# Eighteen early score units, two value units loaded ahead, and cross attention with a PSUM bank for each head

## The reference

```python
def chunk(xc):                                        # PEER: 16384 experts
    q = (xc @ w_query).reshape(PEER_CHUNK, PEER_HEADS, 2, PEER_HALF)
    s1, s2 = ...                                      # scores against 2 x 128 sub-keys
    v1, i1 = lax.top_k(s1, PEER_TOPK)
    v2, i2 = lax.top_k(s2, PEER_TOPK)
    ...
    top, ci = lax.top_k(cand, PEER_TOPK)
    gate = jax.nn.softmax(top, axis=-1)
    act = jax.nn.gelu(jnp.einsum('td,thkd->thk', xc, u))
    return jnp.einsum('thk,thkd->td', gate * act, vv)

def memory_cross_attention(h, m, w_q, w_kv, w_o):     # 4 heads of 256
    s = jnp.einsum('bshd,bmhd->bhsm', q, k) * (XATTN_HEAD_DIM ** -0.5)
    p = jax.nn.softmax(s, axis=-1)
    o = jnp.einsum('bhsm,bmhd->bshd', p, v).reshape(bsz, seq, D_MODEL)
    return jnp.einsum('bse,ed->bsd', o, w_o)
```

## Time and profile before

| what | value |
|---|---|
| median of 3 runs | 2027.73 us (2023.18 to 2029.29) |
| the profiled execution | 2019.04 us, of which the span of its instructions is 2017.4 us |
| PE busy | 1853.8 us (92%) |
| DVE busy | 1341.3 us (66%) |
| ACT busy | 910.5 us (45%) |
| chain that ended last | PE 82%, DVE 9%, ACT 3% of the span |

### The profile page before, as it was taken

The page is one execution under the profiler, slowest core; times in us unless marked ns, Lnnn a source line. Parts: engine busy times, 40 slices in busy tenths (PEclk is TensorE's granted clock), DMA queues, the critical chain, the costliest instruction groups (busy, mean ns, idle before and its releaser), DMA issues.

```text
span 2017.4 us, 25894 instructions
## 1 busy us (share of the span) xinstructions
PE 1853.8 (92%) x10094; PEld 1580.2 (78%) x10094; DVE 1341.3 (66%) x1876; ACT 910.5 (45%) x967; POOL 76.5 (4%) x99
## 2 busy tenths in 40 slices
PE   5999976999799899999999999888977899999997
PEld 3778744788698679999999999787966678878875
DVE  5688775759897555555555555647953478888885
ACT  2543433411233344444444444445543457666664
POOL 0000000000000331110000000000000000000000
PEclk9999997999899999999999999898988899999999
DMA  6655443434345775666555555544334178888892
GB/s 270 240 178 204 149 144 135 167 108 145 116 148 200 236 239 192 213 206 215 186 187 187 187 187 187 197 155 152 126 117 188 55 293 327 327 343 330 319 350 106
DMA packets 60847, 403.93 MB, mean 200 GB/s; under 512 B 7921, under 2 KB 8337, under 8 KB 14305
## 3 DMA queue, kind: packets, MB, share of 16 engines
q1 hardware_dynamic: 51504, 371.22, 50.6%
q0 software_dynamic: 5808, 20.29, 3.4%
q10 hardware_dynamic: 3458, 11.37, 1.7%
HBM read 390.79 MB, written 12.06 MB: 200 GB/s over the span
## 4 chain that ended last, share of the span: by engine, by line
PE 82%; DVE 9%; ACT 3%; issue 3%; DMA 3%; SPq 0%; ACTq 0%; DVEq 0%
PE ps L2152 21%; PE ps L2153 21%; PE ps L2154 21%; PE ps L2254 7%; PE ps L2530 3%; ACT whi L630 2%; DVE wlo L1125 2%; DMA raw<-in_stream_dram 1%; DMA X<-in_x_dram 1%; PE ps L2702 1%; PE ps L2767 1%; PE ps L2589 1%; PE ps L2183 1%; PE ps L2397 1%; PE ps L2629 1%
## 5 line engine op out<-in xcount | busy, mean ns | idle before, releaser
L1125 DVE TENSOR_TENSOR wlo<-raw,whi 128x2048 fp32r<-128x2048 f32 x186 | 429.6, 2310 | 394.0 <-ACT whi L630 394.0
L630 ACT ACTIVATE whi<-raw 128x2048 fp32r<-128x2048 f32 x186 | 356.2, 1915 | 395.0 <-PE ps L2154 372.1
L2152 PE MATMUL ps<-thi,whi 128*128 128x256 f32 x1088 | 310.6, 285 | 9.5 <-DVE wlo L1125 7.0
L2153 PE MATMUL ps<-tlo,whi 128*128 128x256 f32 x1088 | 309.9, 285 | 0.0
L2154 PE MATMUL ps<-thi,wlo 128*128 128x256 f32 x1088 | 309.8, 285 | 0.0
L2152 PE MATMUL ps<-whi,phi 128*128 128x512 f32 x608 | 242.9, 400 | 21.9 <-DVE plo L1705 15.6
L2152 PE MATMUL ps<-whi,thi 128*128 128x512 f32 (+1 forms) x584 | 232.5, 398 | 20.1 <-DVE tlo L1137 11.7
L2153 PE MATMUL ps<-wlo,phi 128*128 128x512 f32 x608 | 240.8, 396 | 0.0
L2154 PE MATMUL ps<-whi,plo 128*128 128x512 f32 x608 | 239.9, 395 | 0.0
L2154 PE MATMUL ps<-whi,tlo 128*128 128x512 f32 (+1 forms) x584 | 228.4, 391 | 0.0
L2153 PE MATMUL ps<-wlo,thi 128*128 128x512 f32 (+1 forms) x584 | 228.1, 391 | 0.0
(11 more groups left out here) (403 smaller groups left out, 2624.2 us busy)
## 6 DMA issues: line engine op xcount, KB each, us to landing
raw<-in_stream_dram SPq DMA_DIRECT2D x264, 1024.0 KB, 4.8
BIG<-in_stream_dram SPq DMA_DIRECT2D x83, 1024.0 KB, 7.0
BIG<-g_spill POOLq DMA_DIRECT2D x64, 128.0 KB, 4.7
BIG<-in_stream_dram SPq DMA_DIRECT2D x2, 2048.0 KB, 15.5
g_spill<-H ACTq DMA_DIRECT2D x4, 1024.0 KB, 4.8
g_spill<-MOD ACTq DMA_DIRECT2D x4, 1024.0 KB, 4.8
MID<-in_gains_dram POOLq DMA_DIRECT2D x7, 512.0 KB, 4.1
s_spill<-MOD ACTq DMA_DIRECT2D x10, 256.0 KB, 4.9
```

The source lines that it names most:

```text
L630: nc.scalar.activation(whi[:, u % 2, :], raw[:, u % 2, :], ACT.Copy).then_inc(unit_hi, 1)
L1125: nc.vector.tensor_tensor(wlo[:, u % 2, :], raw[:, u % 2, :], whi[:, u % 2, :].bitcast(f32), ALU.subtract).then_inc(unit_split, 1)
L2152: nc.tensor.matmul(out, ahi, bhi, start=start, stop=False)
L2153: nc.tensor.matmul(out, ahi, blo, start=False, stop=False)
```

## The change

There are three edits. In all names below, line numbers of the changed kernel differ (L2306 there is L2254 here, L1159 is L1125, L1736 is L1702, L1743 is L1705, L649 is L630, L920 is L899).

First, EARLY goes from 16 to 18. Ten score units (FIRST) now come before the steps that build G, eight between them as before. The ninth and tenth use banks 0 and 1. The tenth is cut in halves, one ahead of the transposes of the routing and one behind; the transposes get three banks. The loop keeps 46 pairs.

Second, the first two value units are loaded into `spare`, which lies in the place of wlo (the allocation is closed at once, so wlo takes the same memory; wlo is idle during the whole units). DVE now multiplies by G ahead of lo, and v(1) is split ahead of phi of v(0).

Third, each head of the cross attention has a bank (4 + h) for its scores, transposes and values in turn, and its own x_p and x_pT. The heads run between the query units and the first W_O unit.

```diff
-EARLY, KEPT = 16, 6
+EARLY, KEPT = 18, 6
+FIRST = EARLY - 8
...
+        with nc.sbuf_tensor("spare", [P, 2, UW], f32) as spare_tensor:
+            spare = spare_tensor
         wlo = sb("wlo", [P, 2, UW], f32r)
...
+        def early_bank(i):
+            return 4 + i % 2 if i < FIRST - 2 else i % 2
...
+        APART = (at_v(0), at_v(1))
...
+                if u in APART:
+                    sp.wait_ge(raw_loaded[u % 2], landed(u - 2))
+                    sp.dma_start(spare[:, u % 2, :], stream[apart[u], :, :]).then_inc(raw_loaded[u % 2], 16)
+                    continue
+                if u - 2 in APART:
+                    sp.wait_ge(raw_loaded[u % 2], landed(u - 2))
+                    sp.wait_ge(unit_used, u - 4 - SPLIT_U + 1)
...
             for i in range(EARLY):
-                if i == 1:
-                    lo(at_v(1))
-                if i >= 2:
-                    lo(at_v(i))
                 if i >= KEPT:
                     dve.wait_ge(s_loaded[(i - KEPT) % 4], 16 * ((i - KEPT) // 4 + 1))
-                gated(i, buffers=(early_out(i), early_out(i)))
+                weighted(i, buffers=(early_out(i), early_out(i)))
+                if i:
+                    lo(at_v(i))
+                weighted_low(i, source=early_out(i))
...
+            for i in range(FIRST - 1):
+                if i >= 2 and early_bank(i) == early_bank(i - 2):
                     pe.wait_ge(gelu_done, i - 1)
-                whole_T(ps[:, 4 + i % 2, :], at_u(i))
-            pe.wait_ge(gelu_done, NE)
+                whole_T(ps[:, early_bank(i), :], at_u(i))
+            whole_T(ps[:, early_bank(FIRST - 1), :], at_u(FIRST - 1), (0, 1))
+            pe.wait_ge(gelu_done, FIRST - 2)
             pe.wait_ge(routed, TT)
             for q in range(3):
-                if q == 2:
-                    pe.wait_ge(route_in, 1)
...
+            whole_T(ps[:, early_bank(FIRST - 1), :], at_u(FIRST - 1), (2, 3))
...
+            group_T(N_XQ, U_XQ, T_HX)
+            group_T(N_XQ + 1, U_XQ + 1)
             x_scores(0)
+            group_T(N_XQ + 2, U_XQ + 2)
             x_scores(1)
+            x_transposes(0)
+            group_T(N_XQ + 3, U_XQ + 3)
+            x_scores(2)
+            x_transposes(1)
+            x_values(0)
+            x_values(1)
+            x_scores(3)
+            x_transposes(2)
+            pe.wait_ge(xo_lo, 2)
+            rows_part(N_XO, U_XO, 0, 0)
+            x_transposes(3)
+            x_values(2)
+            x_values(3)
+            rows_part(N_XO, U_XO, 0, 1)
             pe.wait_ge(xo_lo, XH)
-            for b in range(2):
-                block_rows(N_XO + 2 * b, U_XO + 2 * b, ends=b == 1)
+            block_rows(N_XO, U_XO, units=(1,))
+            block_rows(N_XO + 2, U_XO + 2, ends=True)
```

More of the change, by code:

```diff
@@ L465, in half_cols, with raw_of @@
             return slice(h * 512, (h + 1) * 512)
+        APART = (at_v(0), at_v(1))
+        def raw_of(u):
+            return spare[:, u % 2, :] if u in APART else raw[:, u % 2, :]
         block = ctx.enter_context(nc.Block())
@@ L629, in hi @@
                     act.wait_ge(unit_used, s - 1 + off)
-                nc.scalar.activation(whi[:, u % 2, :], raw[:, u % 2, :], ACT.Copy).then_inc(unit_hi, 1)
+                nc.scalar.activation(whi[:, u % 2, :], raw_of(u), ACT.Copy).then_inc(unit_hi, 1)
             def used(u, off=0):
@@ L1005, in x_out @@
                 nc.scalar.activation(thi[:, 2 * h:2 * h + 2, :].rearrange("p c t -> p (c t)"),
-                                     ps[:, 6 + h % 2, :], ACT.Copy).then_inc(xo_hi, 1)
-            x_exp(0)
-            for i in range(XH * TT):
-                h, t = i // TT, i % TT
-                if i + 1 < XH * TT:
-                    x_exp(i + 1)
-                act.wait_ge(heads_tr, B_HEADS + i + 1)
-                nc.scalar.activation(x_pT[h % 2][:, :, t * P:(t + 1) * P],
-                                     ps[:, 4 + i % 2, 0:S].rearrange("p (k t) -> p k t", k=TT),
-                                     ACT.Copy).then_inc(heads_trT, 1)
-                if t == TT - 1 and h:
-                    x_out(h - 1)
-            x_out(XH - 1)
+                                     ps[:, 4 + h, :], ACT.Copy).then_inc(xo_hi, 1)
+            hi(U_XQ + 2)
+            x_query(0)
+            hi(U_XQ + 3)
+            x_query(1)
+            x_exp(0)
+            hi(U_XO)
+            x_query(2)
+            x_exp(1)
+            x_copy(0)
+            x_query(3)
+            x_copy(1)
+            x_exp(2)
+            x_out(0)
+            x_out(1)
+            hi(U_XO + 1)
+            x_exp(3)
+            x_copy(2)
+            x_copy(3)
+            x_out(2)
+            x_out(3)
             for u in range(U_XO, U_MOE - 2):
@@ L1695, in _, with weighted @@
             dve.wait_ge(g_free, 2 * S // GT)
-            def gated(i, off=0, place=None, buffers=None):
+            def weighted(i, off=0, place=None, buffers=None):
                 place = 2 * (i if place is None else place)
@@ L1703, in gated, with weighted_low @@
                                         G[:, bass.ds(place + 2 * off, 2), :], ALU.mult).then_inc(w_done, 1)
+            def weighted_low(i, off=0, source=None):
+                out = act_w[i % 2] if source is None else source
                 dve.wait_ge(w_hi, i + 1 + off)
@@ L1941, in x_low @@
                 nc.vector.tensor_tensor(tlo[:, 2 * h:2 * h + 2, :],
[L1942 removed]
+                                        ps[:, 4 + h, :].rearrange("p (c t) -> p c t", c=2),
                                         thi[:, 2 * h:2 * h + 2, :].bitcast(f32), ALU.subtract).then_inc(xo_lo, 1)
+            lo(U_XQ + 2)
             x_maxima(0)
[L1946 to L1956 removed]
+            lo(U_XQ + 3)
+            x_weights(0)
+            x_maxima(1)
+            lo(U_XO)
+            x_weights(1)
+            x_maxima(2)
+            x_weights(2)
+            x_low(0)
+            x_low(1)
+            x_maxima(3)
+            x_weights(3)
+            lo(U_XO + 1)
+            x_low(2)
+            x_low(3)
             residual(N_XO, U_XO, 2, 5, 5)
@@ L2619, in _, with x_scores, x_transposes @@
             transposes(T_HX, H)
-            for u in range(4):
-                group_T(N_XQ + u, U_XQ + u, T_HX if u == 0 else None)
-            pe.wait_ge(acc_free, N_XO)
-            def x_scores(i):
-                h, t = i // TT, i % TT
-                if i >= 2:
-                    pe.wait_ge(heads_prob, 4 * B_HEADS + i - 1)
-                for c in range(2):
-                    last = nc.tensor.matmul(ps[:, i % 2, 0:S], xqT[:, 2 * h + c, t * P:(t + 1) * P], kT[:, 2 * h + c, :],
-                                            start=c == 0, stop=c == 1)
-                last.then_inc(heads_scored, 1)
+            def x_scores(h):
+                pe.wait_ge(acc_free, N_XQ + h + 1)
+                for t in range(TT):
+                    for c in range(2):
+                        last = nc.tensor.matmul(ps[:, 4 + h, t * S:(t + 1) * S], xqT[:, 2 * h + c, t * P:(t + 1) * P],
+                                                kT[:, 2 * h + c, :], start=c == 0, stop=c == 1)
+                last.then_inc(heads_scored, 1)
+            def x_transposes(h):
+                pe.wait_ge(x_norm, h + 1)
+                for t in range(TT):
+                    for k in range(TT):
+                        last = nc.tensor.transpose(ps[:, 4 + h, k * S + t * P:k * S + (t + 1) * P],
+                                                   x_p[h][:, t * S + k * P:t * S + (k + 1) * P], ident[:, :])
+                last.then_inc(heads_tr, 1)
             def x_values(h):
-                pe.wait_ge(heads_trT, B_HEADS + TT * (h + 1))
-                if h >= 2:
-                    pe.wait_ge(xo_lo, h - 1)
+                pe.wait_ge(heads_trT, B_HEADS + h + 1)
                 for c in range(2):
```

111 lines of the change are left out of this document (48 added, 63 removed).

## The result

The changed kernel takes 1977.36 us (median of 4 runs, 1971.24 to 1981.22), beside 2028.33 for the kernel before on the same chip: a ratio of 0.9746, 95% interval 0.9722 to 0.977. The forecast was 1980, from 1967 to 1995.

What follows compares the result with a forecast made beforehand. PE, busy 92% of the span, was taken as the bound. Gains of 1.9, 24.7 and 21.3 sum to 47.9 us; 2019.0 profiled gives 1971.1, and with 8.7 from profile to median 1980 us, range 1967 to 1995.

Steps and rivals of the forecast that it cites:

- The loss of 0.2 for the handover: Routing: the ninth unit's Gelu on ACT delays the copies, costing 0.2 us; bounds were nothing and 1.2.
- The first sum, of the early values: Last whole unit to the loop: 107.4 us becomes 105.1 with 18 units, 2.3 less for two units more.
- the restart at half clock: Early values, after the wait ahead of v(0): PE runs at half clock, costing 2.1 us; bounds 1 and 4.
- The second sum, two pairs out of the loop: Loop: two pairs of 11.22 us fewer, a gain of 22.4 us.
- The slack of 0.2 us in the unit's chain: Early values, steady part: a chain of 5.27 us against 5.47 per unit on PE, so no stall is counted.
- the 0.7 taken for a wait: Cross attention: PE waits 0.7 us beyond 61.1, making 61.8; bounds no wait or 4.4, from heads 2 and 3.
- The signs of being wrong: Plo waits returning through the early values, PE waiting for x_norm more than once, or granted clock falling where PE is busy.
- The stall of the early values: Rival: PE still waits once per pair among early values, nine times 1.18, 10.6 us: 1990 us; chance 0.10.
- the heads aren't exposed: Rival denied here: each of four cross attention heads still makes PE wait 2.4 us, 9.6: 1989 us; chance 0.10.
- the two units are hidden: Rival denied here: transposes and one-hot rows slide behind the two units, 13.8 us come back: 1994 us; chance 0.03.
- The transfers' rival: Early values: loads set the pace, 7.0 us per unit, 27 lost: 2007 us; chance 0.04, ending slower 0.03.
- the room of 6.7 us: Early values: a raw buffer goes round in 10.94 us, hi and lo take 4.2, so a landing may take 6.7.

Runs made afterwards that it cites:

- early16: The changed kernel with 16 early units in place of 18, eight of them ahead of the routing: 1987.86 us, ratio 0.9773 to the kernel before.
- after_again: The changed kernel unaltered, run once more for a second profile: 1978.84 us, ratio 0.9736 to the kernel before.
- phi_first: The changed kernel with the split of v(1) put back behind phi of v(0) on ACT: 1977.14 us, ratio 0.9734 to the kernel before.
- early20: The changed kernel with 20 early units in place of 18, twelve ahead of the routing: 1978.45 us, ratio 0.9735 to the kernel before.
- lo_first: The changed kernel with lo again ahead of the multiplication by G on DVE: 1985.29 us, ratio 0.9758 to the kernel before.
- no_spare: phi_first without the spare buffers, so v(0)'s and v(1)'s loads wait for whole units again: 1977.67 us, ratio 0.973 to the kernel before.
- x_only: The kernel before with the third edit (cross attention) alone: 2006.04 us, ratio 0.9869 to the kernel before.
- heads_apart: The changed kernel with the four cross attention heads kept together, no query or W_O unit between their parts: 1984.33 us, ratio 0.9783 to the kernel before.
- tail: phi_first with the seam moved further: last two quarters behind G's last step, v(0) split earlier, its phi ahead of the last Gelu: 1975.1 us, ratio 0.9725.
- order_only: The kernel before with only DVE's multiplication by G put ahead of lo among the early values: 2014.73 us, ratio 0.9924.

## Why the prediction was right, point by point

**The sum.** 47.9 us were forecast; the changed stages give 47.0 and 49.6, the medians 51.0 and 52.4. The medians have the untouched stages in them, which differ between executions by more than the difference that is left; that the measured median, 1977.4, lies within 3 us of the forecast 1980 is partly luck for that reason.

**Edit 1, forecast 1.9.** The stage fell by 2.0 (233.2 to 231.2) and 2.1. The transposes moved by 0.62 (0.6 forecast), and G's first two steps came 3.59 apart (3.51 forecast). The loss of 0.2 for the handover didn't come: the first one-hot row starts, from the first early score unit, where it did (67.32 us, 67.34 before). ACT's three copies start 0.58 us later (66.28 and 65.70), but they end where they did (67.22 and 67.24), since they now run in one piece and the third doesn't wait for a transpose; the prediction had carried over the whole handover of 2.34 as one fixed length. In early16, with its eighth unit halved and two units fewer, PE waits 13.0 us for the routing: that is the idle time which the two units, 13.8 us of matmuls, fill.

**Edit 2, forecast 24.7.** The first sum, of the early values, was 105.1 us; it is 106.9 and 105.7. The wait ahead of v(0) was forecast as 4.45 and is 4.39. A slip in the sum changed nothing: 6.0 less 1.5 is 4.5 and not the 4.2 that was halved for the restart, 0.1 us in the result. Mis-sized were the restart at half clock (TensorE's 1.2 GHz level) and the landings, taken as no wait. Less 4.39 of wait and 18 x 5.47 = 98.5 of units, after_again has 2.8 left where 2.1 were put for the restart; the first profile has 4.0, of which the gap of 1.27 is one part and 2.7 the other. phi_first, whose clock stays at 1.00, has 101.8 - 2.54 - 98.5 = 0.8 left. The second sum, two pairs out of the loop, was 22.4; the stage fell by 24.2 and 23.4, early16 against after_again gives 22.8 and early20 22.6. What goes beyond these came with a granted clock of 0.98 and not 0.97 in it. The slack of 0.2 us in the unit's chain, the weakest number of the prediction, was enough: no wait per pair came back, and lo_first shows that the order on DVE makes it.

Where the gain of edit 2 comes from can be split: the order on DVE 10.1 us (lo_first), the two units 13.8 with the routing's cover (early16), the spare buffers 7.1 where v(0)'s chain is free (no_spare). These overlap and need not add up, since each was taken from a kernel that has the others; each is the difference of two profiles. In the kernel before the order on DVE alone gave 7.8 in its stage.

**Edit 3, forecast 21.3 (61.8 us).** 62.8 and 60.7, in x_only 60.7. The cover sufficed for heads 2 and 3 as well, so the 0.7 taken for a wait was not needed. The first profile's 62.8 has the same records at a granted clock of 0.96: its first 4.8 us, 1490.2 to 1495.0, ran at 0.51 and held 22 matmul records, where the first 4.8 us in after_again held 40 at 1.00. It had fallen before the stage, where eight transposes took 1.77 us (L2235, 1487.69) and not 1.32. heads_apart shows that the cover counted was real.

**The signs of being wrong.** Two of them came in the first profile, small: a wait for plo returned once among the early values (1.27), and the granted clock was at half where PE was busy (the 4.8 us above). after_again has neither. PE never waits for x_norm among the heads.

**The rivals.** The stall of the early values didn't stay, the heads aren't exposed, and the two units are hidden. The transfers' rival is real in kind and small in size: a landing of 8.2 us cost 1.27 in the changed kernel, one of 8.3 cost 1.33 in tail, beside a median landing of 5.0 in that stretch of the changed kernel. Both are over the room of 6.7 us that the prediction gave a landing, by 1.5 and 1.6. That room isn't a sharp bound: the median of tail's five loads was 7.4, so two more were over it, and they cost PE nothing. The rule of the Trainium skill, ScalarE: Activation LUTs, "What ACT_TABLE_LOAD costs", would by the prediction's estimate have made edit 1 lose 1.4 more. Around the routing ACT shows

```profile
531.94 0.31 ACT L869 ACTIVATE MOD<-MOD 128x128 f32<-128x128 f32 x1 [5.92 <-DVE MOD L1700]
532.26 1.28 ACT L879 ACT_TABLE_LOAD   x1
533.56 0.60 ACT L879 ACTIVATE MOD<-ps 128x512 f32<-128x512 f32 x1
```

that is 1.31 us from the Exp's end to the Gelu's start, where that section gives 2.66: the trace does not agree, and nothing was lost. The trace of the kernel before could have told it: there a Gelu ended at 496.61, and the Exp behind its table load started at 497.92, again 1.31 later.

## What to carry to other kernels

Work computed early is free only as long as it fills a wait that is there: by the stages, the first two units beyond sixteen were worth 13.8 us, the next two cost 0.8. Within one engine's queue, put first what another engine waits for: an exchange of two instructions on DVE, in each early value unit, was worth 10.1 us in the changed kernel and 7.8 in the kernel before, and one exchange on ACT, ahead of the first unit, 3.9, of which 1.9 are the wait itself. And when a stage changes by less than the spread of the medians, compare its window in the trace, and subtract the stages that the edit doesn't touch.

## What the runs showed of the hardware

The stage ahead of all edits is the same code in every run and still took from 413.2 us (early20) to 422.7 (lo_first). The windows show where it goes, lo_first and then early20:

```profile
0.00:422.70 422.70, 358.44 (x1631) 273.83 (x1632) 291.80 (x372) 165.52 (x225) 8.48 (x14) 0.94 0.49 180
```

```profile
0.00:413.20 413.20, 348.67 (x1631) 267.37 (x1632) 291.69 (x372) 165.37 (x225) 8.48 (x14) 0.96 0.50 184
```

PE is busy 358.44 and 348.67 us for 1631 records, at a granted clock of 0.94 and 0.96, while DVE is busy 291.80 and 291.69. So the 9.8 us of PE's busy time, as much as an edit here, go with the clock that TensorE is granted in the same code. The clock can also make a wait cost more than its length, and the length alone doesn't say when. After the 4.39 us of idle ahead of v(0), PE's products started 0.42 to 0.43 us apart in all seven profiles that have this wait. After 2.54 us they started 0.23 apart in phi_first, no_spare, order_only and x_only, but in before, after the same 2.54 us, seven products ran at half rate (the first took 0.77 us). In after the half rate lasted about 6 us, from 656.07 to 662.1.
